# A hybrid decoder step: the sample stream scheduled earlier, cache pages loaded in 4 KB pieces, value products over all query columns

## The chip, the cores and the metric

The kernel runs on one core of one Trainium2 chip. The metric is the device time of one execution in microseconds. The kernel before took 1805.47 us as the median of 3 runs (1804.33 to 1810.48).

## What is computed

One decoder layer for a prompt group (512 tokens) and a sample group (8 sequences of one new token each, with 4096 cached positions in pages of 128). All numbers are float32.

```python
# _layer: pre-norm residual; p = RMSNorm(x) @ w_in, split into q, k (4 heads x 2 components x 64), v (4 x 128), conv channels
def _diff_attn_sample(q, k_new, v_new, k_past, v_past, lam):      # k_past, v_past: 32 pages of 128 rows for each sample
    s = jnp.concatenate([_scores(q, k_past), jnp.where(causal, _scores(q, k_new), NEG)], axis=-1)
    a = _diff_weights(s, lam)          # softmax of component 0 minus lam * softmax of component 1
    o_past = jnp.einsum('bhqk,bkhd->bqhd', a[..., :n_past], v_past.astype(jnp.float32))
    o_new = jnp.einsum('bhqk,bkhd->bqhd', a[..., n_past:], v_new.astype(jnp.float32))
    return o_past + o_new
def _layer_tail(x, attn, conv, w_out, norm2_w, router_w, router_b, w_gate_up, b_gate_up, w_down, b_down):
    x = x + jnp.concatenate([attn, conv], axis=-1) @ w_out
    h = _rmsnorm(x, norm2_w).reshape(B * S, D)
    return x + _moe(h, ...)            # 32 experts, top-4 of a softmax router, clamped SwiGLU, D = D_FF = 1024
```

The convolution half is GLU, a causal depthwise convolution of 31 taps, LayerNorm and swish. Outputs are also the new keys, values and convolution states.

## The kernel before

The program has two parts. The **front part** does projection, attention, convolution, output projection and router for 4 prompt tiles of 128 tokens and one "tile" of the 8 sample tokens. The **expert part** walks the 32 experts, streams 12 MB of weights for each through six slots of SBUF and multiplies. It can't start before the router has seen every token, because the tokens of an expert are gathered by the router's tables (`first_tables`, `order_experts`, `gather`).

The front part is cut into pieces with an order written by hand. Each engine has one generator for each piece, and every `plan(...)` line advances one by a stage: P(s) projects tile s, C prepares the convolution weights, Q(j) is prompt attention for one head and one tile, N(s) its head norm, V(half) the convolution taps, L(g) LayerNorm and swish on a range of columns, W(s) the output projection of tile s (plus the residual), and R(s) norm and router for tile s. Tile 0 is the sample rows.

Beside these runs the **sample stream**. A step (b, g) multiplies 2 pages of keys of sample b + 1 by its query (VectorE, L1504) and reduces them to scores (L1507), does the small softmax pieces of sample b, and multiplies value pages of sample b by the exponentials (TensorE, L1337). The number behind each part in `plan` is how many steps are let in behind it (`run_with_samples`). There are 149 steps: in the first 128, two key pages each are read, and the value pages follow some 21 steps later. The stream begins behind P(2). At the start of Q 47 steps are out, at V 83, at W(1) 100, at R(1) 106, at R(2) 117, at R(3) 126. The last 15 lie beside R(4), which has the weight 3.5 for each stage. After that comes the `FINISH` list, with nothing beside it: the last sample's output and its norm (O), L(2) for the 8 sample columns, W(0), R(0). Then come the tables, the first gather and the first expert.

Key and value pages go through rings of four places, each place two pages (512 KB). A page is one DMA of 256 KB on SP's queue: 128 partitions, 2 KB in each (L437). SP issues them in program order: a key load waits for `kred_done` of the place's last user, a value load for `pv_done`. The loads of the first expert's weights (L502, L507) stand behind the whole stream on the same queue. Value products are one product for each head and page: stationary the 2 exponential columns of the head, moving 128 columns of values, into U[32h : 32h+2, 0:128], so that four heads lie on four column groups of the array. `copy_u` (VectorE, L1837) takes U to SBUF, `sample_out` combines the components with one product.

GpSimd splits the experts' bias into bfloat16 parts with 6 instructions (L663 to L668) after `bias_in`; its loads are issued behind O (L1002).

## Time and profile before

| what | value |
|---|---|
| median of 3 runs | 1805.47 us (1804.33 to 1810.48) |
| time of the profiled execution | 1805.06 us |
| its span | 1803.4 us, 1.7 us less than its time |
| mean granted TensorE clock | 0.887 |
| TensorE busy | 1483.9 us, 82% |
| VectorE busy | 802.3 us, 44% |
| ScalarE, GpSimd busy | 331.9 us, 133.2 us |
| moved by DMA | 598.79 MB, mean 332 GB/s |
| expert weights, cache keys and values | 192 loads of 2 MB, 512 loads of 256 KB |

Busy shares are of the whole span. They hide that the front part and the expert part have different limits, so the tables to read are those by stretch. In these the columns are: the stretch in us and its length; then for each engine its busy us and, as (x...), its instructions; the granted clock of TensorE (1 is 2.4 GHz); the share of time in which the 16 DMA engines were busy; and what they moved in GB/s. In a timeline a row is start, length, engine, line, operation, out<-in, count, and in brackets the engine's idle time before it with what ended it. TensorE does a float32 product in two records, so that counts of MATMUL rows are twice the number of products.

### The profile page before, as it was taken

What the parts mean: (1) busy time and instruction counts of PE and PEld (TensorE: products, weight loads), DVE (VectorE), ACT (ScalarE), POOL (GpSimd) and SP (SyncE); (2) the same over time, 40 slices, a digit from 0 to 9 for tenths busy, and PEclk for the clock granted to TensorE, in tenths of its full rate; (3) what the DMA queues carried; (4) which work ended last, traced back from release to release, by engine and by line L of the source; (5) the groups of instructions that cost most, each with busy time, mean ns of one, the idle gap of its engine ahead of it and who ended that gap; (6) DMA issues with size and microseconds to landing.
All of it is one profiled execution on the core that took longest, in us unless ns stands there. A gap on an engine that the chain in (4) does not pass through costs nothing.

```text
span 1803.4 us, 35691 instructions
## 1 busy us (share of the span) xinstructions
PE 1483.9 (82%) x13480; PEld 630.8 (35%) x13481; DVE 802.3 (44%) x1192; ACT 331.9 (18%) x779; POOL 133.2 (7%) x195
## 2 busy tenths in 40 slices
PE   2878966658787864799999999989999999999970
PEld 2434433436443443233333233323323333332320
DVE  3487879995778624312213123321311323232325
ACT  2111111222210001111212112111221211212220
POOL 0000020000000004500000001000000100000100
PEclk8998985679888755799999999999999999899995
DMA  9158898886879784579999999999999999999986
GB/s 334 57 172 258 291 317 264 262 267 207 286 246 293 245 316 155 234 305 406 386 415 426 397 407 427 417 395 407 428 397 408 428 400 412 413 401 397 427 338 243
DMA packets 127887, 598.79 MB, mean 332 GB/s; under 512 B 20935, under 2 KB 20981, under 8 KB 102618
## 3 DMA queue, kind: packets, MB, share of 16 engines
q1 hardware_dynamic: 109088, 560.72, 79.9%
q10 hardware_dynamic: 8522, 20.00, 3.2%
q0 software_dynamic: 10208, 17.11, 2.6%
q8 instruction: 49, 0.80, 0.2%
q14 instruction: 20, 0.16, 0.0%
HBM read 589.89 MB, written 25.90 MB: 341 GB/s over the span
## 4 chain that ended last, share of the span: by engine, by line
PE 39%; DMA 19%; issue 1%; DVE 1%; SPq 0%; ACT 0%; DVEq 0%; ACTq 0%
PE bank L1378 24%; DMA wts<-in_w_gate_up 15%; PE bank L1415 8%; PE bank L1397 4%; DMA wts<-in_w_down 3%; DMA wts<-y_rows 1%; PE bank L1368 1%; PE bank L1464 1%; PE bank L1426 1%; DVE v_ring L1975 0%; DMA h_tok<-h_rows,v_tok 0%; ACT k_T L1036 0%; SPq L555 0%; SPq L566 0%; DVE qk L1922 0%
## 5 line engine op out<-in xcount | busy, mean ns | idle before, releaser
L1378 PE MATMUL bank<-wts,h_T 128*32 128x512 f32 x4096 | 455.1, 601 | 9.7 <-DMA wts<-in_w_gate_up 5.8
L1921 DVE TENSOR_SCALAR q_T<-bank 128x512 f32<-128x512 f32 x32 | 22.1, 692 | 643.4 <-PE bank L1378 643.4
L1378 PEld LDWEIGHTS bank<-wts,h_T 128*32 128x32 f32 x4096 | 132.0, 112 | 318.6 <-issue 307.1
L1415 PE MATMUL bank<-wts,k_T 128*32 128x512 f32 x2048 | 230.5, 599 | 9.5 <-issue 8.3
L1397 PE MATMUL bank<-wts,h_T 128*32 128x512 f32 x1024 | 136.6, 675 | 50.3 <-DMA wts<-in_w_gate_up 48.5
L1504 DVE TENSOR_TENSOR wts<-wts,q_b 128x1024 f32<-128x1024 f32 x128 | 158.2, 1236 | 40.5 <-DMA wts<-in_cache_k 39.4
L1507 DVE TENSOR_REDUCE sc<-wts 128x16 f32<-128x1024 f32 x128 | 156.2, 1220 | 4.4
L1026 ACT ACTIVATE h_T<-bank 128x512 f32<-128x512 f32 x66 | 35.9, 595 | 575.9 <-PE bank L1368 575.9
L1415 PEld LDWEIGHTS bank<-wts,k_T 128*32 128x32 f32 x2048 | 65.4, 111 | 152.2 <-issue 144.6
L1096 PE MATMUL bank<-wts,h_T 128*8 128x128 f32 (+1 forms) x480 | 93.5, 441 | 13.9 <-DMA wts<-in_w_in 7.8
L1337 PE MATMUL bank<-v_ring,ex 128*2 128x128 f32 x2048 | 91.9, 320 | 12.1 <-DMA v_ring<-in_cache_v 12.1
L1036 ACT ACTIVATE k_T<-bank 32x256 f32<-32x256 f32 x256 | 95.9, 374 | 13.1 <-PE bank L1415 9.7
L1096 PE MATMUL bank<-wts,mix 128*128 128x512 f32 x160 | 73.3, 610 | 7.0 <-DVE u_tok L1504 4.8
L1397 PEld LDWEIGHTS bank<-wts,h_T 128*32 128x32 f32 x1024 | 31.3, 117 | 136.2 <-DMA wts<-in_w_gate_up 72.0
L1246 PE MATMUL bank<-wts,mix 128*128 128x512 f32 (+1 forms) x256 | 68.4, 488 | 3.6 <-DVE mix L1504 3.6
L1019 ACT ACTIVATE k_T<-bank 128x512 f32<-128x512 f32 x64 | 34.8, 594 | 187.7 <-PE bank L1464 187.7
L1337 PEld LDWEIGHTS bank<-v_ring,ex 128*2 128x2 f32 x2048 | 49.2, 93 | 54.5 <-issue 27.1
L1140 PE MATMUL bank<-k_T,q_T 64*128 64x128 f32 (+3 forms) x64 | 26.3, 720 | 48.4 <-ACT qk L886 48.4
L1096 PEld LDWEIGHTS bank<-wts,h_T 128*8 128x8 f32 (+1 forms) x480 | 42.2, 141 | 55.8 <-issue 53.9
L1426 PE MATMUL bank<-wts,k_T 128*32 128x256 f32 x1024 | 58.7, 381 | 0.0
L1943 DVE COPY k_T<-bank 64x512 f32<-64x512 f32 x32 | 21.9, 683 | 74.6 <-PE bank L1415 74.1
L1071 PE MATMUL bank<-ident,h_tok 128*128 128x128 f32 (+1 forms) x96 | 16.2, 316 | 41.7 <-DVE h_tok L1530 39.0
(295 smaller groups left out, 1376.7 us busy)
## 6 DMA issues: line engine op xcount, KB each, us to landing
wts<-in_w_gate_up SPq DMA_DIRECT2D x128, 2048.0 KB, 15.1
wts<-in_w_down SPq DMA_DIRECT2D x64, 2048.0 KB, 17.9
wts<-in_cache_k SPq DMA_DIRECT2D x256, 256.0 KB, 3.5
v_ring<-in_cache_v SPq DMA_DIRECT2D x256, 256.0 KB, 3.5
wts<-in_w_in SPq DMA_DIRECT2D x5, 2048.0 KB, 24.0
wts<-y_rows SPq DMA_DIRECT2D x4, 2048.0 KB, 16.0
wts<-in_w_out ACTq DMA_DIRECT2D x1, 4096.0 KB, 19.5
x_in<-in_x_prompt ACTq DMA_DIRECT2D x6, 512.0 KB
```

The source lines that it names most:

```text
L1019: nc.scalar.activation(act_T[part], t_view(TB[part], P), ACT.Copy).then_inc(at_copied, 1)
L1026: nc.scalar.activation(hg_T[:, 4 * q:4 * q + 4, :], t_view(TB[q], P), ACT.Copy).then_inc(xt_copied, 1)
L1036: m = nc.scalar.activation(y_sb[64 + 32 * b:96 + 32 * b, 256 * q:256 * (q + 1)], PS[5][32 * q:32 * q + 32, 256 * b:256 * (b + 1)], ACT.Copy)
L1096: m = nc.tensor.matmul(out, h_T_of(("P", s))[:, kt, 0:n], w_in_sb[:, kt, c0:c0 + cols], start=(kt == 0), stop=(kt == KT - 1))
L1246: m = nc.tensor.matmul(out, mix_T[:, kt, r:r + n], w_out_sb[:, kt, c0:c0 + cols], start=(kt == 0), stop=(kt == KT - 1))
L1337: m = nc.tensor.matmul(U[32 * h:32 * h + C, 0:VD], ex[:, page, C * h:C * h + C], v_ring[:, gg % RING, p, h * VD:(h + 1) * VD], start=(page ...
L1378: m = nc.tensor.matmul(PS[part][p0:p0 + 32, :], lhs[:, 32 * b:32 * b + 32], rhs[:, part * F + half * 512:part * F + half * 512 + 512], sta ...
L1397: nc.tensor.matmul(PS[2 + b][p0:p0 + 32, :], lhs[:, 64 + 32 * b:96 + 32 * b], rhs[:, part * F + half * 512:part * F + half * 512 + 512], s ...
L1415: m = nc.tensor.matmul(PS[4][p0:p0 + 32, :], act_T[0][:, k, a0:a0 + 32], chunk[c][:, k, n * 512:(n + 1) * 512], start=(c == 0 and k == 0), ...
L1426: nc.tensor.matmul(PS[5][32 * q:32 * q + 32, 256 * b:256 * (b + 1)], act_T[1][:, k, a0:a0 + 32], chunk[c][:, k, q * 256:(q + 1) * 256], st ...
L1504: return nc.vector.tensor_tensor(out, a, b, ALU.mult)
L1507: return nc.vector.tensor_reduce(out, src, X, ALU.add)
```

## The change

1. **Schedule.** The stream begins in P(1): 55 steps are out at Q, 91 at V, 117 at L(1), 124 at R(1), 137 at R(2), 149 (all) at the end of R(2)/W(3). The last key step is then in R(1)/W(2). `FINISH` is gone: O lies beside R(3)/W(4), W(0) beside R(4), and R(0) stands alone. L(2) is dropped; the sample's 8 columns are part of L(1) (264 columns instead of 256). The sample's `x` goes to `q_b`, which is free when the keys are done.
2. **Loads.** A page goes to 64 partitions, 4 KB in each: page 0 of a place to partitions 0 to 63, page 1 to 64 to 127.
3. **Value products.** One product for each page: stationary all 8 exponential columns, moving 512 columns, page n to column group n mod 4. Two places are worked off in every second step. The off-diagonal blocks of U are not used; `sample_out` picks the heads with four products instead of one. `copy_u` copies 128x512 on ScalarE. `e_pad` holds the 8 sums four times (one more small copy).

```diff
-            w = 1 if s > 1 else 0
...
-            plan(("P", s - 1), w)
-            plan(("P", s), w)
+            plan(("P", s - 1), 1 if s > 1 else 0)
+            plan(("P", s), 1 if s > 1 else 3)
             if s == 1:
-                plan(("C", 0), 0)
-            plan(("P", s), w)
-            plan(("P", s - 1), w)
-            plan(("P", s), 0, 1, 1, 1)
+                plan(("C", 0), 2)
+            plan(("P", s), 1)
+            plan(("P", s - 1), 1)
+            plan(("P", s), 0 if s > 1 else 1, 1, 1, 1)
...
-        plan(("V", 0), *[1.6] * (CT + 1))
+        plan(("V", 0), *[2.4] * (CT + 1))
         for n in range(CT + 1):
-            plan(("V", 1), 1)
-            plan(("L", 0), 0.8)
+            plan(("V", 1), 1.6)
+            plan(("L", 0), 1.2)
...
-        plan(("R", TILES), *[3.5] * 6)
-        FINISH = [("O", 0)] + [("L", 2)] * 5 + [("W", 0)] * 4 + [("R", 0)] * 6
+        SCHEDULE.append((None, STEPS_ALL))
+        for n in range(4):
+            plan(("R", 3), 0)
+            plan(("W", 4), 0)
+            plan(("O", 0), 0)
+        for n in range(2):
+            plan(("R", 3), 0)
+            plan(("O", 0), 0)
+        for n in range(4):
+            plan(("R", 4), 0)
+            plan(("W", 0), 0)
+        plan(("R", 4), 0, 0)
+        plan(("R", 0), *[0] * 6)
...
-        V_OF_STEP = {V_START: (), V_START + 1: (0, 1), **{V_START + g: (g,) for g in range(2, NG)}}
+        V_OF_STEP = {V_START + g: (g - 1, g) if g % 2 else () for g in range(NG)}
...
-                    sp.dma_start(ring[:, r, p, :],
-                                 cache[bass.ds(page, 1)].rearrange("a p n -> (a p) n")).then_inc(full[r], 16)
+                    sp.dma_start(ring[p * PAGE // GP:(p + 1) * PAGE // GP, r, :, :].rearrange("q j n -> q (j n)"),
+                                 cache[bass.ds(page, 1)].rearrange("a (q j) n -> (a q) (j n)", j=GP)
+                                 ).then_inc(full[r], 16)
...
+            def copy_u(b):
+                act.wait_ge(u_all, b + 1)
+                after(act, ot_done, b)
+                nc.scalar.activation(us[:, :], U[:, :], ACT.Copy).then_inc(us_done, 1)
...
-                nc.tensor.matmul(S7[:, 256 + 4 * b:260 + 4 * b], us[:, :], coef[:, :], start=True, stop=True
-                                 ).then_inc(ot_done, 1)
+                for h in range(H):
+                    m = nc.tensor.matmul(S7[:, 256 + 4 * b + h:257 + 4 * b + h], us[:, h * VD:(h + 1) * VD],
+                                         coef[:, h:h + 1], start=True, stop=True)
+                m.then_inc(ot_done, 1)
...
-                        for h in range(H):
-                            m = nc.tensor.matmul(U[32 * h:32 * h + C, 0:VD], ex[:, page, C * h:C * h + C],
-                                                 v_ring[:, gg % RING, p, h * VD:(h + 1) * VD],
-                                                 start=(page == 0), stop=False)
+                        n = gg * GP + p
+                        q = n % 4
+                        m = nc.tensor.matmul(U[32 * q:32 * q + HC, :], ex[:, n, :], v_ring[:, gg % RING, p, :],
+                                             start=(n < 4), stop=(n >= PAGES - 4 and q > 0))
...
+            def part_o(_s):          # on ScalarE; TensorE and VectorE have their own
+                copy_u(NB - 1)
+                yield
+                yield
+                yield
+                yield
+                act.wait_ge(otsq_done, 1)
+                for q in range(3):
+                    act.dma_start(b_stage[32 * q:32 * q + 32, :], b_gate_up[0]).then_inc(bias_in, 16)
```

## Rows read from the trace of the kernel before

**Rows 1.** Busy time by stretch: P, Q, V and L, then four R/W stretches, O-L-W0, R(0), experts.

```profile
52.00:250.00 198.00, 178.66 (x829) 82.38 (x829) 152.47 (x158) 33.78 (x74) 3.43 (x2) 0.94 0.66 206
250.00:412.00 162.00, 93.40 (x859) 57.71 (x857) 140.96 (x222) 33.66 (x99) 8.39 (x14) 0.65 0.85 279
412.00:485.00 73.00, 59.91 (x1041) 44.18 (x1037) 43.57 (x48) 19.89 (x50) 0.00 (x0) 0.94 0.75 242
...
513.00:560.00 47.00, 33.65 (x250) 17.25 (x242) 39.70 (x62) 3.25 (x9) 0.00 (x0) 0.79 0.89 282
560.00:601.00 41.00, 31.98 (x237) 16.80 (x233) 33.62 (x55) 3.33 (x9) 0.00 (x0) 0.79 0.89 294
601.00:634.00 33.00, 31.80 (x250) 16.89 (x246) 18.91 (x43) 3.54 (x9) 0.00 (x0) 0.86 0.72 227
634.00:671.60 37.60, 26.45 (x277) 16.19 (x269) 8.91 (x32) 3.23 (x8) 0.00 (x0) 0.55 0.89 315
671.60:692.20 20.60, 10.10 (x148) 8.47 (x148) 4.42 (x15) 5.17 (x19) 6.95 (x3) 0.62 0.67 231
692.20:725.70 33.50, 13.11 (x70) 8.58 (x70) 20.82 (x57) 4.90 (x11) 12.24 (x7) 0.53 0.31 123
725.70:1803.40 1077.70, 962.58 (x9024) 335.00 (x9024) 301.46 (x458) 202.21 (x448) 98.91 (x150) 0.95 0.93 390
```

**Rows 2.** VectorE's timeline in R(4), between 633 and 672 us.

```profile
633.95 0.58 DVE L1730 CAST v_tok<-ident 32x32 bf16<-32x32 f32 x3
636.43 1.28 DVE L1530 SCALAR_TENSOR_TENSOR h_tok<-rot,stn,norm_b 128x1024 f32<-128x1024 f32 x1 [1.91 <-ACT stn L746]
...
652.20 0.19 DVE L1501 TENSOR_TENSOR logit<-bank,r_b 128x32 f32<-128x32 f32 x1 [13.95 <-PE bank L1271]
...
663.31 0.29 DVE L1504 TENSOR_TENSOR q_T<-q_T,bank 128x128 f32<-128x128 f32 x1 [6.88 <-PE bank L1285]
```

**Rows 3.** VectorE's timeline in R(0), the same two places.

```profile
703.63 0.18 DVE L1501 TENSOR_TENSOR logit<-bank,r_b 8x32 f32<-8x32 f32 x1 [2.46 <-PE bank L1271]
...
711.21 0.28 DVE L1504 TENSOR_TENSOR q_T<-q_T,bank 8x128 f32<-8x128 f32 x1 [3.51 <-PE bank L1285]
```

**Rows 4.** Timeline of GpSimd and VectorE, 684 to 704 us.

```profile
685.10 1.89 POOL L663 CAST u_T<-v_ring 96x2048 bf16<-96x2048 f32 x1 [274.52 <-DMA v_ring<-in_b_gate_up]
...
692.15 4.04 DVE L1730 CAST v_tok<-ident 32x32 bf16<-32x32 f32 x3
...
696.23 4.96 DVE L1530 SCALAR_TENSOR_TENSOR h_tok<-x_in,stn,norm_b 8x1024 f32<-8x1024 f32 x1
700.17 2.76 POOL L668 CAST u_T<-v_ring 32x2048 bf16<-32x2048 f32 x1
```

**Rows 5.** DMA of 320 to 350 us: packets, and SP's queue.

```profile
DMA packets 4464, 8.14 MB, mean 271 GB/s; under 512 B 498, under 2 KB 498, under 8 KB 4463
...
q1 hardware_dynamic: 4463, 8.12, 84.6%
```

**Rows 6.** DMA of 900 to 945 us, expert weights: packets.

```profile
DMA packets 1723, 18.71 MB, mean 416 GB/s; under 512 B 438, under 2 KB 438, under 8 KB 629
```

**Rows 7.** VectorE's groups, 412 to 485 us: busy, mean ns, idle before and its cause.

```profile
L1504 DVE TENSOR_TENSOR wts<-wts,q_b 128x1024 f32<-128x1024 f32 x16 | 19.5, 1222 | 20.0 <-DMA wts<-in_cache_k 19.8
```

**Rows 8.** TensorE's timeline, 97 to 218 us.

```profile
97.72 6.53 PE L1096 MATMUL bank<-wts,h_T 128*128 128x512 f32 x8 [5.82 <-DVE u_tok L1504]
...
186.71 0.62 PE L1337 MATMUL bank<-v_ring,ex 128*2 128x128 f32 x16
187.26 3.70 PE L1096 MATMUL bank<-wts,mix 128*128 128x512 f32 x8
...
217.04 0.39 PE L1306 MATMUL bank<-coef,us 128*128 128x4 f32 x2
```

**Rows 9.** TensorE's groups, 1000 to 1100 us, four column groups side by side.

```profile
L1378 PE MATMUL bank<-wts,h_T 128*32 128x512 f32 x488 | 53.8, 599 | 0.0
```

**Rows 10.** DMA of 680 to 683 us: ScalarE's queue (the bias loads), packets, MB, share.

```profile
q10 hardware_dynamic: 147, 0.77, 102.6%
```

More of the change, by code:

```diff
@@ L272, in hybrid_step @@
         used, stage_of = {"A": 0, "T": 0}, {}
-        for part in [p for p, _w in SCHEDULE] + FINISH:
+        for part in [p for p, _w in SCHEDULE if p]:
             n = stage_of.get(part, 0)
@@ L291, in hybrid_step @@
         row0 = [SEQ] + [n * P for n in range(TILES)]
-        v_rows = [v_samp[:, :]] + [v_tok[:, n, :] for n in range(TILES)]
+        v_rows = [v_samp] + [v_tok[:, n, :] for n in range(TILES)]
         kc = cache_k[0].rearrange("n p h c d -> n p (h c d)")
@@ L305, in hybrid_step @@
         v_full = [sem(f"v_full{n}") for n in range(RING)]
-        xw_loaded = [sem(f"xw_loaded{n}") for n in range(2)]
+        xw_loaded = [sem(f"xw_loaded{n}") for n in range(TILES + 1)]
         win_in = [sem(f"win_in{n}") for n in range(5)]
@@ L386, in run_with_samples @@
             for part, weight in SCHEDULE:
-                next(stages[part], None)
+                if part:
+                    next(stages[part], None)
                 due += weight
                 while due >= 1:
-                    for b, g in [x for x in [next(steps, None)] if x]:
-                        step(b, g)
-                    due -= 1
-            for b, g in steps:
-                step(b, g)
+                    nxt = next(steps, None)
+                    due = due - 1 if nxt else 0
+                    if nxt:
+                        step(*nxt)
         w_slot = [wts[:, n * SLOT:(n + 1) * SLOT] for n in range(6)]
@@ L993, in sample_step @@
                                          ).then_inc(exp_done, 1)
+                if 0 < b < NB and g == 5:
+                    copy_u(b - 1)
+            def copy_u(b):
[11 more added lines that the diff above has]
+                    act.dma_start(b_stage[32 * q:32 * q + 32, :], b_gate_up[0]).then_inc(bias_in, 16)
+                rstd(sto[:, 0:32], sto[:, 32:64], S7[:, 288:320], 1.0 / VD, otr_done)
+                yield
+                yield
             parts = {"P": part_p, "C": part_c, "Q": part_q, "N": part_n, "V": part_v, "L": part_l, "W": part_w,
[L996 removed]
+                     "R": part_r, "O": part_o}
             stages = {part: parts[part[0]](part[1]) for part in a_no if part[0] in parts}
             run_with_samples(sample_step, stages)
[L1000 to L1005 removed]
             act.preload_act_table_set("sigmoid_and_others")
@@ L1342, in sample_step @@
                     pe.wait_ge(vn_in, 16 * (b + 1))
-                    for h in range(H):
-                        m = nc.tensor.matmul(U[32 * h:32 * h + C, 0:VD], ex[0:1, PAGES, C * h:C * h + C],
-                                             v_new[0:1, h * VD:(h + 1) * VD], start=False, stop=True)
-                    m.then_inc(u_all, 1)
+                    nc.tensor.matmul(U[0:HC, :], ex[0:1, PAGES, :], v_new[0:1, :], start=False, stop=True
+                                     ).then_inc(u_all, 1)
             pe.wait_ge(pool_consts, 1)
@@ L1350, in _ @@
             parts = {"P": part_p, "C": part_c, "Q": part_q, "N": part_n, "V": part_v, "L": part_l, "W": part_w,
-                     "R": part_r}
+                     "R": part_r, "O": part_o}
             stages = {part: parts[part[0]](part[1]) for part in a_no if part[0] in parts}
             run_with_samples(sample_step, stages)
-            sample_out(NB - 1)
-            pe.wait_ge(otss_done, 1)
-            nc.tensor.matmul(M[:, 448:480], ones[:, :], ot_sq[:, :], start=True, stop=True).then_inc(otsq_done, 1)
-            for part in FINISH[1:]:
-                next(stages[part], None)
             TB = [PS[6], PS[7]]
@@ L1817, in sample_step @@
                         ).then_inc(sub_done, 1)
-                if 0 < b < NB and g == 5:
-                    copy_u(b - 1)
                 if 0 <= b < NB and g == 5:
```

116 lines of the change are left out of this document (62 added, 54 removed).

## The prediction, made before the changed kernel was run

> **What bounds the kernel now.** I read the table of stretches first [rows 1], since the page's shares mix two parts. The last stretch, from the first expert product at 725.7 us to the end, is 1077.7 us with TensorE busy for 962.6 of them at a clock of 0.95 and the DMA engines busy 93% of the time. The change touches nothing in it, so I carry it over as it is: what the change is worth is by how much it moves 725.7.
>
> The front part has three limits, one after the other. In P (52 to 250) TensorE is busy for 178.7 of 198 us, its order of projection and value products setting the pace. In Q (250 to 412) VectorE is: 141.0 of 162 us, while TensorE runs at 0.65 of its clock. From 412 to 601 neither is full; VectorE works off key steps (up to 39.7 of 47 us) between the router's small operations, and the DMA engines are up to 89% busy. From 634 on the front part is a chain of small dependent operations: in 634 to 671.6 TensorE still does value products of the last sample, in 671.6 to 692.2 O, L(2) and W(0) follow one another with every engine mostly idle (TensorE 10.1 of 20.6), and R(0) takes 33.5 us more at half clock. These last three stretches are 91.7 us, with little besides latency in the last two.
>
> **The tail.** The change takes O, L(2) and W(0) off the end, and puts them beside R(3)/W(4) and R(4).
> - O, L(2), W(0) standing alone: 20.6 us go [rows 1]. What hides them: O's dozen small operations lie in R(3)/W(4), where VectorE is busy for only 18.9 of 33 us; W(0)'s products lie in the gaps of R(4). I charge 3 us for W(0) in TensorE's and ScalarE's order. Without that cover the whole 20.6 us come back.
> - R(4) without value products: VectorE waited 13.95 us for the logits and 6.88 for the rank [rows 2]; in R(0), where nothing lies between, the same two waits are 2.46 and 3.51 [rows 3]. The difference is 14.9 us; the products of 128 instead of 8 rows keep about 2 of it, so 12.8 go. 37.6 - 12.8 + 3 = 27.8 us for R(4) with W(0): -9.8.
> - The bias split: GpSimd's six instructions run from 685.1 to 702.9 [rows 4], and VectorE's three casts and its norm take 4.04 and 4.96 us beside them against 0.58 and 1.28 in R(4) [rows 2, 4]. The idle time hides part of the 7.1 us this costs; about 6.5 lie on R(0)'s path, and R(0) gets them back. But the loads of the bias are now issued within R(3), so the same six instructions meet R(4), whose path has more VectorE operations. Bounds: 0 if they fall wholly into R(3)'s slack, 17.8 us if VectorE stands still for all of it. I take 9, by the 7.1 that two operations have cost, and a third one caught. Net +2.5.
> - R(3)/W(4) without the nine steps: TensorE is busy for 31.8 of 33 us, some 6 of them value products and their neighbours. But with less to do the clock is likelier to sit at its lower level: eight projection records take 3.70 us at the high one, and up to 6.53 in the stretch at 97.7 us [rows 8]; four such groups make W(4), so up to +11. I take -2 net.
> - Sum of the tail: -20.6 - 9.8 + 2.5 - 2 = -29.9 us.
>
> **The steps that move forward.** 23 steps that lay beside or behind R(3) must go somewhere. Eight go to P, nine more (26 instead of 17) to V and L, the others mostly into R(1) and R(2).
> - P: a key step is 2.4 us of VectorE (1.22 for the product [rows 7] and as much for the reduction); eight more are 20 us, and VectorE is idle for 45 of P's 198. Eight value groups more cost TensorE 8 x 0.55 = 4.4 us (start to start of the rows at 186.71 and 187.26 [rows 8]). Against it stands what part 3 saves; 0, between -4 and +5.
> - Q: as many steps as before on a VectorE that is full. `copy_u` leaves it, a small copy comes: 0. Fewer or shorter records on a slow TensorE: -3, between -6 and +3.
> - V and L: nine steps more in 73 us. VectorE has room (43.6 + 9 x 2.4 = 65 us), TensorE too (59.9 + 9 x 0.5 = 64.4). DMA is the limit: 26 steps are 27.3 MB. In 320 to 350 us, where almost all traffic is 2 KB rows of the cache, 8.14 MB took a share of 0.849 of 30 us, so the engines at 100% carry 320 GB/s, and a packet costs 16 x 0.846 x 30 us / 3965 = 102 ns [rows 5]. Expert weights, mostly in packets over 8 KB, go at 390 / 0.93 = 419 GB/s [rows 1, 6]. A 4 KB packet lies between; a fixed cost and a cost for each byte through 2 KB at 320 and 16 KB at 419 give 370. 27.3 MB are 74 us by that and 85 us at 320. VectorE already waited 19.8 us there for keys, with DMA at 75% [rows 7], so the ring isn't smooth: I take 79, +6, between 0 and +15.
> - R(1)/W(2): only 4 key steps instead of 11, so 7 x 2.4 = 17 us of VectorE go, where it was busy for 39.7 of 47 us; TensorE then sets the pace with 33.7 us of work plus two value groups: 47 to 41, -6. R(2)/W(3): VectorE 33.6 of 41 us, no key step left: 41 to 36, -5. Between -18 and 0 together. W(1): -1.
> - Sum before R(3): 0 - 3 + 6 - 1 - 6 - 5 = -9 us.
>
> **Value products.** The columns are the same: before, two pages are 16 records of 128 columns, 0.55 us; now four pages are 8 records of 512. Such records, four column groups side by side, take 53.8 us for 488 in the experts, 110 ns each [rows 9], so 0.88 us against 1.11 for four pages: 64 x 0.23 = 15 us of TensorE in all, in stretches where mostly another engine is late. `sample_out` has four products instead of one, each with a load of 128 columns: one costs 0.39 us with two records [rows 8], so up to 8 x 1.2 = 9 us back. `copy_u` costs ScalarE under 1 us a sample (its 99 operations in Q average 0.34 us [rows 1]); it waits there for the sample's last value product, and the exponentials of Q, which VectorE needs, queue behind that wait. Net 0, between -5 and +5. If the four groups did not overlap, a page would be worth two projection records, 0.93 us: 256 x (0.93 - 0.28) = 166 us; but the experts' rows show overlap in the same form, and I leave it at 2 in 100.
>
> **Sum.** The profiled execution took 1805.1 us, 0.4 below the median of the runs, so it stands for them. 1805.1 - 29.9 - 9 = **1766.2 us**.
>
> **Rival 1, slower: a page in half the partitions.** All 16 engines now write one page into 64 partitions. The trace has one case like it, the bias loads (32 partitions each, 8 KB rows): in 680 to 683 us their queue keeps the engines at 102.6%, and moves 0.77 MB, 257 GB/s [rows 10], against 419 for wide loads. A factor of 0.61; on 370 it makes 227. For it: this row. Against it: the two pages of a place go to opposite halves, key and value places follow each other, and engines that have drifted apart don't meet. The price at 227: P's 55 key and 34 value groups are 46.7 MB, 206 us instead of 198, +8; Q's 72 groups 37.7 MB, 166 us, +4; V and L 120 us, +41 over my 79; W(1) 7.3 MB, 32 us, +4: 1766 + 57 = 1823 us. It decides below about 240 GB/s, where V and L alone take 114 us; the rest of the gain of 39 us goes with P and W(1). At 257, 106 us, some 1794. Chance of slower by this, with the 2 in 100 above: 20%.
>
> The Trainium skill speaks for it ("SBUF — State Buffer", the sections on the DMA port swizzle and on issuing two DMAs to hit both halves): partitions 0 to 63 reach only 8 of 16 ports, 196 GB/s at 1 MiB against 328, and a second DMA on the other half gives 6% more. By an estimate from that page, 134 MB of cache at about 208 GB/s would take 645 us, and the kernel would end near 1880. The row of the bias loads agrees in kind; no row shows two halves in turn.
>
> **Rival 2: given back before R(3).** The tail gains, but V and L take 90 us (ring waits, as the 19.8 us [rows 7]: now a value load waits for a product that runs every second step, and the key loads queued behind it on SP wait too), and R(1), R(2) gain only 4 because the router's chain and not VectorE was late: 1766 + 11 + 7 = 1784; with P +5 and Q +3, 1792. Chance 15%: 7% for 1786 to 1800, 8% above, short of slower.
>
> **Rival 3: the tail at half clock.** W(4) at the lower level +11, the bias split 17.8 instead of 9: 1786. It stays inside the likeliest case's own range; chance 10%.
>
> **Rival 4: a larger gain.** DMA was late in more places than the waits show, and R(1) to R(3) lose all their gaps: 1745 or below. 10%. That the change does nothing measurable (1800 to 1811) needs rivals 2 and 3 together; these are the 8% of rival 2.
>
> **Chances.** The forecast, with rival 3 in it, 1746 to 1786: 55%. With rival 4 (10%) and the first part of rival 2 (7%) faster by over 0.3% has 72%, within 0.3% 8%, slower 20%. 0.3% is about what a measurement of this kernel can tell from no change. The range for 8 in 10 must take in the bounds of V and L, of the clock and the upper part of the given-back case, but not the whole of rival 1: 1744 to 1815.
>
> **What the profile after would show.** The first expert product near 687 us; no key wait longer than before in V and L; R(1)/W(2) and R(2)/W(3) near 41 and 36 us with VectorE mostly idle in the second; R(4) with W(0) about 37 us including the bias split, and the casts of 4 us there and not in R(0). Rival 1 shows as a DMA share near 1 at 230 to 260 GB/s from 150 us on, and long waits for cache keys and values in P and Q. Rival 2 shows as V and L at 90 us with DMA below 90%. The forecast is wrong if the expert part doesn't stay at 1078 us, or if value products take over 0.3 us a page at the high clock.

## The result: 1899.0 us, slower by 5.2%, and the profile after

The changed kernel takes 1899.0 us (median of 4 runs, 1893.3 to 1901.4) against 1804.9 for the kernel before beside it: a ratio of 1.0517, 95% interval 1.0475 to 1.0559. The forecast was 1766.2 with a range up to 1815. The profiled execution has a span of 1895.1 us.

The table of stretches of the changed kernel, which answers to [rows 1] and has its columns. The first three rows end with the first product of attention, of the convolution and of the first output projection; the last two begin with the norms of R(4) and R(0) and end with the next norm and the first expert product. By the same marks the kernel before has 198.6, 161.4 and 77.7 us in the first three ([rows 1] end V and L some 5 us earlier, at 485).

```profile
52.00:286.36 234.36, 195.02 (x578) 80.56 (x578) 177.83 (x185) 36.51 (x79) 6.57 (x3) 0.90 0.88 212
286.36:479.26 192.90, 105.89 (x412) 50.67 (x408) 140.11 (x222) 33.99 (x100) 5.23 (x13) 0.57 0.96 230
479.26:601.48 122.22, 88.61 (x921) 49.56 (x917) 69.30 (x72) 20.37 (x51) 0.00 (x0) 0.80 0.99 227
...
762.13:796.02 33.89, 16.79 (x173) 11.61 (x173) 21.18 (x32) 5.38 (x17) 14.55 (x5) 0.60 0.40 156
796.02:823.62 27.60, 13.11 (x70) 8.59 (x70) 13.21 (x53) 4.91 (x11) 1.70 (x3) 0.50 0.11 35
```

The first expert product comes at 823.6 us instead of 725.7; the expert part takes 1071.5 us instead of 1077.7. All of the loss lies ahead of R(3)'s norm, which comes at 730.1 us and not at 601.7: projections +35.7 us, attention +31.5, convolution +44.5, from there to the norm +16.7. From that norm to the first expert product it is 93.5 us, against 124.0 before: the tail gained 30.5.

The page points to the loads. Its DMA row (40 slices of 47 us, busy share in tenths) stands at 9 from some 140 to 660 us, at 210 to 267 GB/s, and two groups have grown a long idle time (section 5 of the page: busy time, mean ns, idle time before and its cause). VectorE's key product waited 39.4 us for keys before, TensorE's value products 12.1 us for values.

```profile
DMA  9589999999999976339899999999999999999985
GB/s 303 139 207 248 239 222 267 220 225 220 210 239 227 235 190 248 126 132 389 347 412 417 427 406 415 383 427 412 401 415 429 389 412 414 428 390 411 427 356 232
...
L1537 DVE TENSOR_TENSOR wts<-wts,q_b 128x1024 f32<-128x1024 f32 x128 | 158.1, 1235 | 155.4 <-DMA wts<-in_cache_k 149.1
...
L1379 PE MATMUL bank<-v_ring,ex 128*8 128x512 f32 x512 | 108.6, 761 | 45.9 <-DMA v_ring<-in_cache_v 45.9
```

The DMA view of 300 to 330 us answers to [rows 5]: at a share of 0.99 in all (q1 and q10) the engines carry 7.34 MB in 30 us, 245 GB/s. Before, 0.85 carried 271.

```profile
DMA packets 2160, 7.34 MB, mean 245 GB/s; under 512 B 369, under 2 KB 369, under 8 KB 2159
...
q1 hardware_dynamic: 1790, 5.89, 81.3%
q10 hardware_dynamic: 369, 1.45, 17.4%
```

SyncE's timeline around 435 us (start, duration, form, number of loads) shows something I had not read before the prediction: without any wait, the two pages of a group are issued every 2.14 us, and the two issues themselves take 1.14 of it.

```profile
430.04 1.13 SPq L449 DMA_DIRECT2D wts<-in_cache_k  x2
432.19 1.14 SPq L449 DMA_DIRECT2D v_ring<-in_cache_v  x2
434.40 1.18 SPq L449 DMA_DIRECT2D wts<-in_cache_k  x2
```

Two pages are 0.524 MB, so at this distance SyncE issues 245 GB/s; in the kernel before the median distance is 1.87 us, 280 GB/s, and about two thirds of its groups lie no further apart.

### The profile page after: what moved, and what is told of

Same layout as the page of the kernel before. It is cut to its first block, busy times and chain, and to the rows that moved or that the text cites. A ratio compares the mean times of both kernels' runs of the same rounds, so it can differ in the third digit from the quotient of the medians.

```text
span 1895.1 us, 32590 instructions
## 1 busy us (share of the span) xinstructions
PE 1525.7 (81%) x11928; PEld 606.1 (32%) x11929; DVE 807.8 (43%) x1184; ACT 333.5 (18%) x778; POOL 132.9 (7%) x201
## 4 chain that ended last, share of the span: by engine, by line
PE 43%; DMA 26%; SPq 15%; DVE 8%; issue 6%; POOL 1%; ACT 1%; DVEq 0%; ACTq 0%; POOLq 0%
PE bank L1411 21%; DMA wts<-in_w_gate_up 14%; SPq L449 8%; PE bank L1448 7%; DMA wts<-in_cache_k 5%; SPq L446 5%; PE bank L1430 3%; DMA wts<-in_w_down 3%; PE bank L1126 2%; DVE wts L1537 2%; PE bank L1379 2%; DMA wts<-in_w_in 2%; DVE sc L1540 1%; DMA v_ring<-in_cache_v 1%; PE bank L1275 1%
## 5 line engine op out<-in xcount | busy, mean ns | idle before, releaser
L1379 PE MATMUL bank<-v_ring,ex 128*8 128x512 f32 x512 | 108.6, 761 | 45.9 <-DMA v_ring<-in_cache_v 45.9
L1275 PE MATMUL bank<-wts,mix 128*128 128x512 f32 (+1 forms) x256 | 74.2, 515 | 5.5 <-DVE mix L1877 5.5
L1126 PEld LDWEIGHTS bank<-wts,mix 128*128 128x128 f32 x160 | 31.6, 203 | 47.1 <-issue 47.0
```

Source lines behind the costliest of these rows:

```text
L1126: m = nc.tensor.matmul(out, h_T_of(("P", s))[:, kt, 0:n], w_in_sb[:, kt, c0:c0 + cols], start=(kt == 0), stop=(kt == KT - 1))
L1275: m = nc.tensor.matmul(out, mix_T[:, kt, r:r + n], w_out_sb[:, kt, c0:c0 + cols], start=(kt == 0), stop=(kt == KT - 1))
L1379: m = nc.tensor.matmul(U[32 * q:32 * q + HC, :], ex[:, n, :], v_ring[:, gg % RING, p, :], start=(n < 4), stop=(n >= PAGES - 4 and q > 0))
```

## The experiments

The runs fall into five groups, each on a chip of its own with runs of the kernel before beside it. That kernel took 1822 us in the first group, 1804, 1807 and 1803 in the next three and 1825 in the last, so only ratios to it are compared between groups, and stretches only ahead of the first expert product. All ratios below are to the kernel before. No changed kernel ran on two chips, so small differences between groups rest on the ratio carrying over. Three theories stood at the start: **A**, the set of partitions limits a load (rival 1); **B**, a load of 64 rows of 4 KB is slow by itself, whichever partitions it writes; **C**, the loads are not the cause, but the order of waits is, with value groups in pairs and key loads queued behind them (part of rival 2). A fourth came with SyncE's timeline: **I**, SyncE's own issue time bounds the loads. The letters S, D, E, M, N, J, K and F are explained where they are first expected.

### The load by itself

A kernel that computes nothing and only issues page loads from SyncE, in five forms: 128 partitions of 2 KB; 4 KB in half the partitions, halves in turn; 4 KB in every second partition; one half alone; two adjacent pages in 128 partitions of 4 KB.

> No kernel of the layer: it only loads 256 KB pages of the key cache, in eight stages one after the other, and computes nothing. Stages: 32 pages to 128 partitions with 2 KB each; 32 pages to alternating halves of 64 partitions with 4 KB each; 32 pages to every second partition with 4 KB each; 16 pages all to partitions 0 to 63; 16 loads of two adjacent pages to 128 partitions with 4 KB each; then halves, every second, wide again. Theory A (the set of partitions limits a load: partitions 0 to 63 are reached by half of the ports, and two loads to opposite halves go one after the other): wide about 320 GB/s, halves and one half both 210 to 240, every second and the adjacent pairs 350 to 385. Theory B (a load of 64 rows of 4 KB is slow by itself): halves, every second and one half all 210 to 240, only the pairs fast. Theory C (loads are not the cause at all; the order of waits in the changed kernel is): halves 350 or more.

The forms by stretch, in the order wide, halves in turn, every second partition, one half, adjacent pairs (clock, DMA share, GB/s at the end of a line):

```profile
2.00:23.00 21.00, 0.00 (x0) 1.00 1.03 368
28.00:62.00 34.00, 0.00 (x0) 1.00 1.04 231
66.00:88.00 22.00, 0.00 (x0) 1.00 0.98 365
92.00:110.00 18.00, 0.00 (x0) 1.00 1.03 213
114.00:132.00 18.00, 0.00 (x0) 1.00 1.02 412
```

Halves in turn carry 231 GB/s with every engine busy, hardly more than one half (213). Three forms came a second time in the same execution: halves in turn 232, every second partition 373, wide 371. The 4 KB piece is not at fault, so B is out: in every second partition, also 64 of them, it reaches 365, and in all 128 even 412. What counts is which partitions one load writes. This is the mechanism of rival 1, and near its rate (227 there). The Trainium skill ("SBUF — State Buffer", "Can I just issue two DMAs to hit both halves?") says that a second load on the other half adds 6%; here it adds 8%, and the trace agrees.

### Wide pages in the changed kernel, halves in the kernel before

```diff
 # changed kernel, wide pages (the second run: the same lines the other way round in the kernel before)
-sp.dma_start(ring[p * PAGE // GP:(p + 1) * PAGE // GP, r, :, :].rearrange("q j n -> q (j n)"),
-             cache[bass.ds(page, 1)].rearrange("a (q j) n -> (a q) (j n)", j=GP)
-             ).then_inc(full[r], 16)
+sp.dma_start(ring[:, r, p, :],
+             cache[bass.ds(page, 1)].rearrange("a p n -> (a p) n")).then_inc(full[r], 16)
```

> The changed kernel with the pages loaded as before (128 partitions, 2 KB each); schedule and value products stay. Theories A and B: the 98 us by which the first expert product came later than before vanish and the gain of the tail shows: 1765 to 1785 us, first expert product at 685 to 705 us, DMA share in P and Q back at 0.7 to 0.85. Theory C (value groups in pairs, and key loads queued behind them on SP): it stays near 1880 to 1900 us.

> The kernel before with only the loads changed (page n to half n mod 2, 4 KB in each partition). Theories A and B: slower than before by about as much as the sample stream's loads last longer: 134 MB at 230 to 240 GB/s are 560 to 585 us; with the tail of before behind it 1880 to 1930 us. Theory C: within 10 us of before.

Wide pages: 1.0091 (1.0061 to 1.0121), 1839 us. Halves in the kernel before: 1.0397 (1.0366 to 1.0427), 1894 us. So the halves cost 4.3% in the changed kernel and 4.0% in the kernel before, 72 to 77 us, the largest part of the loss. The second run came out as A and B expected. The first is a miss for all theories: A and B wanted 1765 to 1785 us, C 1880 to 1900. The forecast's gain is not what is left: the changed kernel with wide pages is still 0.9% slower than before, so something of C or of rival 2 holds beside A.

### Pages on every second partition, and SyncE's part in it

```diff
-ring[p * PAGE // GP:(p + 1) * PAGE // GP, r, :, :]
+ring[p::GP, r, :, :]
```

> The changed kernel with page 0 of a place on the even and page 1 on the odd partitions, still 64 partitions with 4 KB each for one page; keys and values have the same order, so the result is the same. Theory A: the loads reach all ports again, 1755 to 1780 us, not slower than with 128 partitions of 2 KB. Theory B: stays at 1890 to 1900 us. Theory C: the same, 1880 to 1900.

1.0250 (1.0207 to 1.0293): 2.6% better than halves and 1.6% worse than wide, though the load by itself was as fast. This is the cleanest measure of A: SyncE's groups lie 2.15 us apart here as with halves, and only the set of partitions differs. But the time is 1869 us where A had expected 1755 to 1780, and the DMA share in attention is 0.75 only. Theory I was tested with one edit of SyncE, made in eight kernels: the page numbers of four groups are read from SBUF at once.

```diff
-sp.load(page_regs, pages_sb[0:1, bass.ds(first_page, GP)])      # in load_pages: for each group of 2 pages
...
+sp.load(regs_of[x], pages_sb[0:1, bass.ds(first_page, N8)])      # in read_pages: for 4 groups, x "k" or "v"
```

> The kernel before with one edit: SyncE reads the page numbers of four groups (8 pages) at once into 8 registers for keys and 8 for values, instead of 2 for each group. Theory I (SyncE's own issue time is what bounds the cache loads: in its timeline the loads of one group start a median of 1.87 us after those of the group before, 0.524 MB, 280 GB/s, at 70% of all groups without a wait, of which the two issues are 0.86 us): the median distance falls to 1.4 to 1.7 us, VectorE's 40 us of waits for keys fall to under 25, and the time by 8 to 30 us, to 0.983 to 0.996 of before. Rival J (the DMA engines, with a share of 0.85 in the attention part, or the consumers bound it, and SyncE merely keeps step): the distance falls but the time stays within 3 us.

> The changed kernel with the same edit of SyncE alone (page numbers read for four groups at once). In the changed kernel the groups start 2.14 us apart (245 GB/s), 1.15 us of it the two issues, and the load-only run gave 231 GB/s for halves in turn at a full share. Theory A (half the partitions, half the ports: the DMA engines bound it at 231 GB/s): the time stays between 1888 and 1902 although SyncE is faster, with waits of SyncE for free places instead. Theory I alone (the halves cost only because a 64-row load takes 0.15 us longer to issue): 1840 to 1865.

> The changed kernel with pages on every second partition (4 KB pieces, all ports) and page numbers read for four groups at once. Theory I (what these pages still cost over wide ones is SyncE's issue period of 2.15 us, 244 GB/s, against 1.87): the period falls to some 1.46 us and the time from 1.025 of before to 1.000 to 1.010. Rival (the pages themselves are slower in the company of other traffic): 1.018 to 1.028.

> The changed kernel with wide pages and batched page numbers, to be compared with the run of pages on every second partition and batched numbers (1.0149). If the page's form costs nothing beside SyncE's issue time: 1.008 to 1.014. If each page on every second partition is slower of itself: 0.994 to 1.003, the 1.2% that batching gave elsewhere off the 1.0091 of wide pages.

The kernel before with it: SyncE's timeline shows 1.16 us from group to group,

```profile
340.61 0.86 SPq L440 DMA_DIRECT2D wts<-in_cache_k  x2
341.77 0.85 SPq L440 DMA_DIRECT2D v_ring<-in_cache_v  x2
342.94 0.85 SPq L440 DMA_DIRECT2D wts<-in_cache_k  x2
```

a median of 1.2 instead of 1.87, and the time is 0.9922 (0.9899 to 0.9946), within the range expected by I. The convolution part fell from 79.2 to 71.2 us. Two things came out otherwise than expected. VectorE's waits for keys only fell from 39.7 to 34.8 us, and SyncE's waits for value products rose from 47.3 to 107.5: much of the time that SyncE saved it now waits for free places. And the median fell below the 1.4 to 1.7 us expected. In SyncE's records one read of two page numbers takes 0.47 us and one of eight 0.75, so the reads themselves are 0.28 us of the 0.67 that a group saves; the rest is register arithmetic and gaps around them. (The Trainium skill, "DMA: Bandwidth & Descriptors", "Latency and other measured facts", has about 0.6 us as the least for such a read; the 0.47 measured here is below it, and the measurement decides.)

The changed kernel with it: 1.0575 (1.0550 to 1.0601), 1910 us and so even above the range of A, in any case no faster though SyncE's distance fell from 2.14 to 1.46 us. There the DMA engines are the limit, as A says; their share in attention is 0.94 at 220 GB/s. The wide one with it: 1.0003 (0.9990 to 1.0017), 0.9% less than without; every second partition: 1.0149 (1.0118 to 1.0180), 1.0% less than without, where I had expected 1.5% to 2.5%. So SyncE's issue time bounds part of every version except the one with halves, and the last run came out as the expectation had it for pages that are slower of themselves. But that test was not clean. The same edit does not make SyncE's distance the same: in the run with every second partition, and then in the one with wide pages, SyncE has

```profile
317.18 1.14 SPq L452 DMA_DIRECT2D v_ring<-in_cache_v  x2
318.62 1.14 SPq L452 DMA_DIRECT2D wts<-in_cache_k  x2
```

```profile
311.40 0.85 SPq L452 DMA_DIRECT2D v_ring<-in_cache_v  x2
312.57 0.86 SPq L452 DMA_DIRECT2D wts<-in_cache_k  x2
```

The medians are 1.46 and 1.20 us with the edit and 2.15 and 1.87 without it, so the gap between the two forms hardly changed, as the gap in time hardly did (1.5% and 1.6%). Whether the longer issue of the 64-row loads costs it or something else in the form is open; no run has the two forms at one distance.

### The value products and the groups in pairs

```diff
 # one group a step, as before, in the changed kernel with wide pages
-V_OF_STEP = {V_START + g: (g - 1, g) if g % 2 else () for g in range(NG)}
+V_OF_STEP = {V_START: (), V_START + 1: (0, 1), **{V_START + g: (g,) for g in range(2, NG)}}
 # and then also the products of before: four of 128 columns a page, copy_u on VectorE, one product in sample_out
```

> The kernel before, unchanged, profiled on the chip on which the next three run, so that stretches are compared on one chip. Both theories expect the stretch lengths of the first profile within 2%: 199 us from 52 us to the first attention product, 161 to the first convolution product, 78 to the first output projection, 180 from there to the first expert product minus 57.6+33.4 in the last two parts, and 40 us of waits of VectorE for key pages (x128 multiplies). If instead this chip is slower by 15 to 20 us, as the times of before in the last call were (1822 against 1805), the stretches say where, and that part is no effect of any edit.

> The changed kernel with two parts undone: pages of 128 partitions x 2 KB, as before, and the value groups one a step instead of two every second step. Theory S (a second loss beside the page's halves: SyncE issues key and value loads in one order, and with two groups at a time the load of a value page waits for the products longer, with key loads queued behind it; in the run with wide pages SyncE waited 69.0 us for value products, against 47.4 in before): SyncE's wait for value products falls to 45 to 55 us, VectorE's wait for key pages from 80.8 us to 40 to 60, and the time falls by 20 to 35 us from 1839, to 1804 to 1819, that is 0.98 to 0.99 of the run with wide pages alone and level with before or under it. Rival D (demand: more steps are asked for ahead of the output projection than the loads can bring, whatever their order): the waits only change their owner, and the time stays within 8 us of 1839.

> As the last one, and with the value products of before too (four of 128 columns a page, four column blocks of U, U copied by VectorE, one product a row for the output): what is left of the change is the order of the steps and the tail. Theory S, as it stands, gives the products nothing: within 5 us of the last run. Rival E (the value products with all query columns cost time: in the wide run TensorE was busy 1506 us against 1484 in before, a value page took 1.04 us at the high clock and 1.90 at the low): 6 to 20 us less than the last run. Rival D: within 8 us of 1839 in both.

> The kernel before with one part of the change alone: one value product a page with all 32 query columns (8 x 512 with weights of 8 columns), U in one row block for every fourth page, four small products for a row's output. Theory S: 0 to +4 us against before. Rival E: +6 to +20 us against before, above all in the stretches of attention, convolution and projections, where TensorE is busiest. A gain of more than 3 us would be against both.

The kernel before repeated its stretches within 2% here (first expert product at 728.0 us, 1805.6 us in all). One group a step: 1.0031 (1.0012 to 1.0051) against 1.0091 with pairs, and SyncE's wait for value products went from 69.0 to 48.9 us, VectorE's for keys from 80.8 to 59.7. The waits are about as theory S had them. The time, 1810 us, also lies in its range, but not for its reason: S had compared with 1839 us on the slower chip of the first group, and by the ratios the gain is 0.6%, 11 us, and not 20 to 35. With the products of before as well 0.9989 (0.9966 to 1.0012), another 0.4%; that is 8 us, as rival E had it. The products alone in the kernel before: 1.0163 (1.0129 to 1.0196), 29 us by the ratio, beyond even rival E.

TensorE's timeline shows why pairs and products belong together. The changed kernel (start, duration, records; two for each page now, 8 before):

```profile
215.08 1.04 PE L1379 MATMUL bank<-v_ring,ex 128*8 128x512 f32 x8
...
222.00 1.03 PE L1379 MATMUL bank<-v_ring,ex 128*8 128x512 f32 x4
```

The kernel before, with the new products alone, and as it was:

```profile
190.14 1.03 PE L1341 MATMUL bank<-v_ring,ex 128*8 128x512 f32 x4
194.73 1.03 PE L1341 MATMUL bank<-v_ring,ex 128*8 128x512 f32 x4
```

```profile
192.75 0.62 PE L1337 MATMUL bank<-v_ring,ex 128*2 128x128 f32 x16
196.14 0.62 PE L1337 MATMUL bank<-v_ring,ex 128*2 128x128 f32 x16
```

Four pages in four column groups take 1.04 us; two pages in two column groups take 1.03. (The row at 222.00 has only two pages because the other group of its pair still waited for its load and came at 225.52.) From start to start, a group of two pages costs 0.96 us (190.14 and 191.10) against the old 0.55 [rows 8], and only a pair of groups makes it up: 0.98 us (192.07 and 193.05 in the changed kernel) for four pages against 1.10. The pairs in turn cost 0.6% net, with longer waits of SyncE for value products, and together the two edits cost 1.0%.

### Where the steps lie

The schedule of the change alone, with wide pages and old products, is level with before (0.9989), although its tail, from R(3)'s norm to the first expert product, is 95.5 us against 125.7. Four orders were compared, all with wide pages and the products of before.

```diff
 # late steps: weights of before up to R(2)/W(3), no early start, then
+for s in range(1, 4): 4 x [plan(("R", s), 2.5 if s == 3 else 1); plan(("W", s + 1), same)]; plan(("R", s), 1, 1)
+SCHEDULE.append((None, STEPS_ALL))
+3 x [O, R(4), O], then W(0), R(4), W(0), W(0), R(4), W(0), R(4), then R(0)
```

The early start was added to the late steps by the weights of P(1) and C of the change, with 1.5 instead of 2.5 beside R(3)/W(4).

> Wide pages and the value products of before; the order of the steps is that of before up to R(2)/W(3) (no step earlier in P, V or L), the 22 steps that are left (value pages alone, no key) lie beside R(3)/W(4), then O beside the first half of R(4) and W(0) beside its second half. So it has the tail of the change without the steps that the change moves ahead of R(3). Theory M (what moves ahead of R(3) costs there about 1.6 us a step, which ate the 30 us of the tail; in the schedule-only run R(3)'s norm stood at 638.6 us against 602.4 in before): R(3)'s norm at 600 to 604 us, R(3)/W(4) 33 us by TensorE or up to 42 by the loads of 22 value groups at 1.87 us each on SyncE, R(4) with O and W(0) 34 to 38, R(0) 28; first expert product 700 to 712, time 1774 to 1788, 0.983 to 0.991 of before. Rival N (the tail gains only because all value work is over before R(3) begins): first expert product at 720 or later, 1795 or more.

> The late-steps kernel (wide pages, products of before, 22 steps beside R(3)/W(4)) with one part put back: the key steps start two router tiles earlier, as in the change, so 8 steps move from R(3)/W(4) into the projections. Theory K (the early start isn't free: in 75 to 125 us VectorE is busy 24.5 of each 25 us, so that the norms of the next tiles and with them TensorE's projections come later): the first attention product 15 to 27 us later than in the late-steps run (251), the first convolution product 10 to 15 later (412), R(3)/W(4) 10 shorter (54.7), time within 6 us of the late-steps run or up to 8 slower. Rival F (it is free, as forecast: VectorE idle for 45 of 198 us): first convolution product within 4 us of 412, and 8 to 12 us faster than the late-steps run.

> The late-steps kernel of this call and the batched page numbers together. Theories M and I: the two gains add, 1755 to 1775 us, with the stretch from the convolution to R(3) shorter too. If only M holds 1774 to 1788, if only I holds 1780 to 1800.

> The schedule of the change with wide pages and the value products of before, and page numbers read for four groups at once. Theory I (the fuller convolution part took 104 us instead of 79 because SyncE issues no more than 280 GB/s): that stretch falls to 80 to 90 us, R(3)'s norm from 638.6 us to 610 to 622, time 1772 to 1787. Rival D (VectorE and TensorE are what is full there): the stretch stays at 98 us or more, time 1793 to 1802.

> The late-steps kernel with batched page numbers, and part of the 22 late steps moved forward: 5 more in the convolution part, 2 or 3 in R(1) and R(2), 16 beside R(3)/W(4); no early start. If with the shorter issue period the convolution part has room (theory I), it takes 76 to 80 us instead of 71.7, R(3)/W(4) falls from 53.3 to 42 to 46, and the time is 1768 to 1778, the best so far. If each step costs the same wherever it lies: within 3 us of 1780.

> The late-steps kernel with the early start (0.9849 of before) and batched page numbers. Theory I and K together: the batched numbers took 1.1% off the late-steps kernel and 1.2% off the schedule-only kernel, so 0.972 to 0.978, 1752 to 1764 us, first expert product at 682 to 694. Rival: early start and batched numbers buy the same thing (keys earlier), so together no more than one of them: 0.982 to 0.986.

First the schedule of the change, its first three stretches (projections, attention, convolution), then the late steps, then late steps with the early start (projections, attention, convolution, R(3)/W(4)):

```profile
52.00:276.33 224.33, 187.38 (x986) 86.79 (x986) 181.84 (x188) 34.82 (x76) 9.48 (x4) 0.90 0.72 236
276.33:425.61 149.28, 96.16 (x845) 59.11 (x841) 132.60 (x216) 33.02 (x98) 2.32 (x11) 0.61 0.87 281
425.61:529.63 104.02, 78.36 (x1234) 56.26 (x1234) 69.99 (x73) 19.78 (x50) 0.00 (x0) 0.83 0.83 261
```

```profile
412.31:490.25 77.94, 65.74 (x1084) 48.29 (x1081) 48.74 (x52) 19.89 (x50) 0.00 (x0) 0.90 0.79 247
...
603.90:658.58 54.68, 43.26 (x450) 22.91 (x443) 19.04 (x45) 3.66 (x10) 0.00 (x0) 0.81 0.79 258
```

```profile
52.00:271.96 219.96, 186.06 (x986) 86.35 (x986) 180.65 (x185) 34.83 (x76) 9.48 (x4) 0.91 0.74 240
271.96:419.98 148.02, 99.48 (x844) 60.73 (x841) 132.50 (x216) 33.01 (x98) 2.31 (x11) 0.59 0.87 281
419.98:498.17 78.19, 67.10 (x1080) 49.78 (x1080) 46.74 (x51) 19.77 (x50) 0.00 (x0) 0.91 0.75 235
...
601.90:637.34 35.44, 33.35 (x331) 18.25 (x334) 10.45 (x33) 3.12 (x8) 0.00 (x0) 0.89 0.81 274
```

- Late steps: 0.9958 (0.9940 to 0.9975), 1797.8 us, a miss for theory M, which wanted 1774 to 1788. R(3)'s norm came at 603.9 as it said, but 22 value groups beside R(3)/W(4) made that stretch 54.7 us instead of 33.0, beyond the 42 I had allowed, and the first expert product at 730.3 us is no earlier than in the kernel before. What it gained lies in the expert part: 1068.4 us, against 1076.7 in the kernel before with batched numbers on the same chip. Why is open.
- The early start added to it: 0.9849 (0.9820 to 0.9878). Attention begins 21 us later, but the convolution only 7.7, and R(3)/W(4) is 19.2 us shorter. Both theories missed: the early start is not free, but it is worth 1.1%, more than either gave it.
- So it is the other half of the move, 10 more steps in the convolution part and W(1), and the rest in R(1) and R(2) instead of beside R(3), that ate the tail: schedule of the change 0.9989, the same early start with late steps 0.9849, a difference of 1.4%. (The two also differ in O, which stands beside R(3)/W(4) in the first and beside R(4) in the second.) The convolution part took 104.0 us with them and 78.2 without.
- Batched page numbers take 1.2% off the schedule of the change (0.9869, 0.9848 to 0.9891; with its time and R(3)'s norm, 612.4 us, as theory I expected, but its convolution part at 93.6 us and not at 80 to 90), 1.1% off the late steps (0.9851, 0.9826 to 0.9876; 1779.8 us, 5 us above the range expected, where theory I alone would have it), and 0.6% off late steps with the early start: 0.9793 (0.9762 to 0.9824), between what theory and rival had given, with the first expert product at 699.3 us and not at 682 to 694.
- An even spread, with batched numbers: 0.9883 (0.9862 to 0.9904), no better than late steps with them (0.9851); the rival had it. Its convolution part took 86.2 us, not 76 to 80.

Late steps, early start and batched page numbers together, wide pages and the old products: 2.1% faster than before and the best of all. Of the change it keeps only the early start and the tail, with O moved to R(4).

## Why the prediction was wrong, point by point

**The tail was right.** -30.5 us against -29.9, and -30.2 with the schedule alone; the three stretches each came within 3 us. VectorE's waits for logits and rank in R(4) are 6.24 and 0.40 us instead of 13.95 and 6.88 [rows 2]; R(4) with W(0) and the bias split is 33.9 us (36.8 forecast), R(0) 27.6 (27.0), R(3)/W(4) 32.0 (31). The bias split moved as forecast: the casts take 3.97 us and the norm 5.14 in R(4), as they did in R(0) before [rows 4].

```profile
766.06 3.97 DVE L1763 CAST v_tok<-ident 32x32 bf16<-32x32 f32 x3
770.07 5.14 DVE L1563 SCALAR_TENSOR_TENSOR h_tok<-rot,stn,norm_b 128x1024 f32<-128x1024 f32 x1
781.45 0.19 DVE L1534 TENSOR_TENSOR logit<-bank,r_b 128x32 f32<-128x32 f32 x1 [6.24 <-PE bank L1300]
...
787.21 0.29 DVE L1537 TENSOR_TENSOR q_T<-q_T,bank 128x128 f32<-128x128 f32 x1 [0.40 <-PE bank L1314]
```

**The step that failed is the rate of a page.** V and L were charged at 370 GB/s, from a law of packet size drawn through two points [rows 5, 6], when the one row of a load that wrote part of the partitions [rows 10] gave 257 GB/s at a full share. The law was right that larger packets carry more, though both its figures were low (368 GB/s at 2 KB, 412 at 4 KB in 128 partitions); the set of partitions decided. Halves in turn carry 231 GB/s by themselves, and in the kernel V and L carried 227 at a share of 0.99 and took 122 us, where 79 was forecast. The arguments set against rival 1 (opposite halves in turn, drifting engines) are refuted by the load-only run: 231 against 213. Rival 1's 227 was right within 2% partly by luck: against the 412 of wide 4 KB pieces the factor is 0.56 and not 0.61, and it was put on 370. Its signs came true: from 150 us to the end of the projections the engines are full at 238 GB/s, and V and L took about its 120 us.

```profile
150.00:286.36 136.36, 113.88 (x358) 44.34 (x356) 92.58 (x95) 20.58 (x40) 6.57 (x3) 0.91 1.00 238
```

Its time of 1823 us was too low. It priced DMA alone in four stretches and left the gains of R standing. It spread P's loads over the whole of P, though the engines carried only 104 GB/s up to 75 us and 147 up to 100; P took 234 us, not 206. Q took 192.9 us, 27 more than its 166. And it counted Q as +4 where the forecast that it adds to already had -3: some 4 us more are missing in its sum, with W(1).

**The row of the share was read as room.** [rows 5] show the engines at 0.85 in a stretch where SyncE issues most groups without a wait. I read 15% room for nine more steps in V and L; but 271 GB/s is near what SyncE issues at 1.87 us a group (280). The term for V and L, +6 and at most +15, fails even without halves: with the schedule alone the convolution part grew by 25 us, from 79.2 to 104.0. SyncE's distance is only a small part of that. With batched page numbers in both it still grows by 22, from 71.2 to 93.6, though the distance is 1.2 us. What bounds the added steps there is not shown.

**P was not free.** It was forecast at 0, at most +5. VectorE idle for 45 of 198 us is a mean [rows 1]; in 75 to 125 us it is busy for 45 of 50 in the kernel before. The changed kernel, and then the kernel before, from 100 to 125 us:

```profile
100.00:125.00 25.00, 17.16 (x49) 8.94 (x50) 24.52 (x27) 3.13 (x6) 0.00 (x0) 0.72 0.92 230
```

```profile
100.00:125.00 25.00, 25.00 (x67) 11.72 (x66) 22.01 (x21) 5.42 (x12) 0.00 (x0) 0.98 0.65 201
```

TensorE falls from 25.0 to 17.2 us of work and its granted clock from 0.98 to 0.72, while VectorE is busy for 24.5 us of the 25. The halves are not the reason: late steps without and with the early start, both with wide pages, show the same.

```profile
100.00:125.00 25.00, 25.00 (x64) 11.55 (x63) 20.59 (x20) 4.70 (x9) 0.00 (x0) 0.92 0.60 177
```

```profile
100.00:125.00 25.00, 17.95 (x48) 8.68 (x49) 24.02 (x25) 2.68 (x6) 0.00 (x0) 0.80 0.79 260
```

That the next tile's norm stands behind key work is the likely way; it was not tested by itself. Attention gets most of it back; the start alone costs 7.7 us at the convolution, and pays 7.7 in R(2)/W(3) and 19.2 in R(3)/W(4).

**Value products: right for four pages, wrong in company.** 0.98 us from start to start (0.88 forecast from [rows 9], 1.11 before), but only with four pages at a time. That SyncE's queue stands behind pairs was in rival 2, with its mechanism, and is worth 0.6%. Rival 2 held beside rival 1: with wide pages the convolution part is still 102.4 us, and single groups (102.6) don't shorten it. I had let the two exclude one another.

The loss taken apart along one chain of runs, in per cent of before: order of the steps -0.1, products +0.4, pairs +0.6, halves +4.3. That they make 5.2 together is arithmetic, since each is the difference of two neighbours in the chain, each known to 0.2 to 0.5. In another order they come out otherwise: in the kernel before the halves alone cost 4.0 and the products alone 1.6. The first is itself a tail of -30 us and +36 ahead of it.

## What to carry to other kernels

Here a load's rate was set first by the set of partitions that it writes, so price a load by a row of a load of that shape, however short, and not by the size of its packets. A DMA share below 1 need not be room: look at the issuing engine's timeline before more loads are asked of it, and where it issues back to back take the reads of addresses out of its loop (worth 0.6 to 1.2% in every version but the one with halves). A stretch that is asked to take work off a chain is read in windows of 25 us and not in the mean of 200.

## What the runs showed of the hardware

- 64 partitions as one half: 213 GB/s; halves in turn: 231; every second partition, also 64: 365; 128 at 2 KB: 368; 128 at 4 KB: 412.
- SyncE's record of one load with its address in a register is 0.33 us for 128 rows and 0.47 us for 64 rows twice as long (0.86 and 1.14 from the first to the end of the second); a read of two page numbers is 0.47 us, one of eight 0.75.
- Value products with weights of 8 columns, 512 columns long: four pages in four column groups take 1.04 us, two pages in two column groups 1.03. The overlap of the experts' rows [rows 9] pays only where all four are issued together.
- Open: why pages on every second partition cost 1.5% beside other work and nothing by themselves. SyncE's longer issue (1.46 against 1.20 us a group) is a candidate.
